# A fourth lead unit in the second auxiliary PSUM pair, and a new order of the work around the leads of four FFNs

## The reference, cut to what matters

```
def swiglu(x, wg, wu, wd):
    return (jax.nn.silu(x @ wg) * (x @ wu)) @ wd

x = x + 0.5 * swiglu(rms_norm(x, n_ffn1[i]), w_ffn1_gate[i], w_ffn1_up[i], w_ffn1_down[i])
mix, v, new_buf, hT = hybrid_mix(rms_norm(x, n_mix[i]), ...)
x = x + mix
x = x + 0.5 * swiglu(rms_norm(x, n_ffn2[i]), w_ffn2_gate[i], w_ffn2_up[i], w_ffn2_down[i])
gate = jax.nn.sigmoid(rms_norm(x, n_ple[i]) @ w_ple_gate[i])
x = x + gate * (p @ w_ple_proj[i])
```

## Time and profile before

| | |
|---|---|
| median of 3 runs | 1858.75 us (1858.49 to 1860.04) |
| the profiled execution: time | 1858.88 us |
| its span, from the first to the last instruction | 1857.2 us |
| mean granted TensorE clock | 0.994 of full speed |
| PE busy | 1819.7 us, 98% of the span |
| DVE busy | 1508.2 us, 81% |
| ACT busy | 1063.0 us, 57% |

### The profile page before, as it was taken

The page is one execution under the profiler, slowest core; times in us unless marked ns, Lnnn a source line. Parts: engine busy times, 40 slices in busy tenths (PEclk is TensorE's granted clock), DMA queues, the critical chain, the costliest instruction groups (busy, mean ns, idle before and its releaser), DMA issues.

```text
span 1857.2 us, 37525 instructions
## 1 busy us (share of the span) xinstructions
PE 1819.7 (98%) x14824; PEld 1797.5 (97%) x14824; DVE 1508.2 (81%) x2319; ACT 1063.0 (57%) x1538; POOL 299.4 (16%) x380
## 2 busy tenths in 40 slices
PE   7999999999999999999999999999999999999997
PEld 6999999998999999999999999999999999999997
DVE  7989978768689889787689789777775897988775
ACT  6656656545456566565466565554544665655553
POOL 0011011340120110112110110115202101011122
PEclk9999999999999999999999999999999999999998
DMA  5657579722346666795355765794223657667941
GB/s 173 155 151 188 136 199 246 216 80 69 110 134 155 175 166 152 194 262 172 124 148 127 197 167 158 209 249 147 71 92 114 162 137 194 158 160 230 237 140 47
DMA packets 81265, 297.16 MB, mean 160 GB/s; under 512 B 9344, under 2 KB 11680, under 8 KB 79312
## 3 DMA queue, kind: packets, MB, share of 16 engines
q1 hardware_dynamic: 52592, 184.87, 30.9%
q0 software_dynamic: 28512, 110.03, 27.8%
HBM read 267.00 MB, written 25.74 MB: 158 GB/s over the span
## 4 chain that ended last, share of the span: by engine, by line
PE 89%; DVE 7%; issue 2%; ACT 1%; DMA 0%; DVEq 0%; SPq 0%; ACTq 0%
PE main L764 24%; PE main L730 19%; PE main L769 12%; PE aux L764 9%; PE main L926 9%; PE aux L769 5%; PE aux L926 4%; PE aux L1028 2%; PE main L819 2%; PE aux L730 1%; PE aux L976 1%; DVE w_lo L1690 1%; PE main L1028 1%; PE aux L1048 0%; DVE tmp L1854 0%
## 5 line engine op out<-in xcount | busy, mean ns | idle before, releaser
L764 PE MATMUL main<-part_hi,w_hi 128*128 128x260 f32 x1296 | 328.5, 284 | 8.8 <-DVE tmp L1854 5.3
L764 PE MATMUL main<-part_lo,w_hi 128*128 128x260 f32 x1296 | 326.6, 283 | 0.0
L764 PEld LDWEIGHTS main<-part_hi,w_hi 128*128 128x128 f32 x1296 | 244.5, 189 | 11.6 <-DVE tmp L1854 7.7
L764 PEld LDWEIGHTS main<-part_lo,w_hi 128*128 128x128 f32 x1296 | 244.5, 189 | 0.0
L622 POOL DMA_DIRECT2D w_lo<-weights_dram x104 | 90.3, 868 | 851.1 <-ACT w_lo L1154 842.5
L769 PE MATMUL main<-part_hi,w_lo 128*128 128x260 f32 x1296 | 213.7, 282 | 0.2 <-DMA w_lo<-weights_dram 0.2
L1166 ACT ACTIVATE w_hi<-tau 128x1024 fp32r<-128x1024 f32 x104 | 109.9, 1057 | 177.0 <-PE main L769 152.4
L730 PE MATMUL main<-part_hi,w_hi 128*128 128x260 f32 x944 | 192.6, 285 | 2.0 <-DVE tmp L1738 2.0
L730 PE MATMUL main<-part_hi,w_lo 128*128 128x260 f32 x944 | 189.8, 283 | 0.0
L730 PE MATMUL main<-part_lo,w_hi 128*128 128x260 f32 x944 | 189.5, 282 | 0.0
L764 PE MATMUL main<-sig,w_hi 128*128 128x260 f32 x1280 | 181.6, 284 | 5.7 <-issue 5.7
(11 more groups left out here) (325 smaller groups left out, 4544.1 us busy)
## 6 DMA issues: line engine op xcount, KB each, us to landing
raw<-weights_dram SPq DMA_DIRECT2D x344, 512.0 KB, 3.8
w_lo<-weights_dram POOLq DMA_DIRECT2D x104, 512.0 KB, 6.4
d_part<-tmp POOLq DMA_DIRECT2D x64, 260.0 KB, 5.3
x<-d_part POOLq DMA_DIRECT2D x16, 1040.0 KB, 14.3
x_spill<-x POOLq DMA_DIRECT2D x6, 1040.0 KB, 4.9
x<-x_spill POOLq DMA_DIRECT2D x6, 1040.0 KB, 9.8
x<-x_in_dram SPq DMA_DIRECT2D x4, 520.0 KB, 6.7
x<-tmp POOLq DMA_DIRECT2D x4, 520.0 KB, 3.2
```

The lines of the kernel that those rows point to most:

```text
L764: pe.matmul(ps, hi_w[:, w], xx(k), start=(start and k == 0 and b == 0), stop=False, skip_group_check=True)
```

## The change

Four things change in the leads and in the first chunk of each FFN.

1. Unit 3 of the lead goes to `aux[1]` (the new list `FOURTHS`). PE waits ahead of it for `root` (`std_s`) and not for `gate_out(0)`. The `main` pairs shift by one, so that P1(0) takes the pair of unit 0 and P1(1) that of unit 1. The wait for `hidden_out(1)` moves from P1(1) to the first down product.
2. On ACT `copy_p1(0)` stands right behind `hi12`, and `h_lead(1)` behind `copy_p5(0)`.
3. On DVE `hidden_out(1)`, `tau3`, `tau4` and `hidden_lo(0)` leave the lead and stand behind `lo12`: `lo12`, `tau3`, `tau4`, `hidden_out(1)`, `lo34`, `hidden_lo(0)`, `lo_b`. `hidden_lo(1)` goes behind `lo12` of the second tile. The copy of the lead's two hidden tiles into x (POOL's queue) becomes two DMAs of one tile each, each behind its own `hidden_out`.
4. The first chunk's sums of pair 0 are made behind tile 0 and not behind tile 2, and the low part of pair 1 moves from tile 1 to tile 2.

```diff
+FOURTHS = tuple(t + 1 for t in THIRDS)
...
-SUM_ORDER = ((1, 0, 2, 3), (0, 1, 2, 3))
...
-    return (g + layer + (k >= G_GT + V_AFTER) + sum(g > t for t in THIRDS)) % 2
+    return (g + layer + (k >= G_GT + V_AFTER) + sum(g > t for t in THIRDS + FOURTHS)) % 2
...
-            return aux[0] if g in THIRDS else main[main_slot(g)]
+            return aux[0] if g in THIRDS else aux[1] if g in FOURTHS else main[main_slot(g)]
...
-            def copy_lead(f, G):
-
-                pool.wait_ge(evac, G)
+            def copy_lead(f, G, k):
+
+                pool.wait_ge(evac, G - 2 * (LEAD - 1 - k))
...
-                pool.dma_start(x[:, XT - 2:XT, :], tmp[:, 2:4, :]).then_inc(lead_copy, 16)
+                pool.dma_start(x[:, XT - LEAD + k, :], T(2 + k)).then_inc(lead_copy[k], 16)
...
                     weights_in(n + 3)
-                    pe.wait_ge(evac, G + 1)
+                    pe.wait_ge(std_s, stat + 1)
                     acc(bank(G + 3), 3, XT, x_hi, x_lo).then_inc(unit, 1)
...
                         if first and t < 2:
-                            pe.wait_ge(evac, G - 2 * (1 - t))
+                            pe.wait_ge(evac, G - 3 + t)
...
-                        if t == 1:
+                        if c and t == 1:
                             pe.wait_ge(evac, G)
...
-                            pe.wait_ge(std_s, stat + 1)
+                            pe.wait_ge(evac, G)
...
                         hi12(n, S)
+                        copy_p1(0)
                         hi34(n, S)
                         act.wait_ge(sx_lo, 2 * KH * (2 * l + which + 1))
                         hi_b(n, S)
-                        h_lead(l, G - 2 * LEAD, 1)
...
-                    copy_p1(0)
+                    if c:
+                        copy_p1(0)
                     copy_p1(1)
                     gate(2)
                     copy_u2(0)
                     copy_p5(0)
+                    if first:
+                        h_lead(l, G - 2 * LEAD, 1)
...
-                            ahead(1, S0, S)
-                            ahead(2, S0, S)
-                            hidden_lo(0)
-                            hidden_out(1)
+                            tau1(S0, S)
+                            tau2(S0, S)
...
-                        if first and t == 2:
+                        if first and t == 0:
                             sums_raw(f, c, 0)
                             sums_raw2(f, c, 0)
...
-                        if not last and t >= pairs and k % 2:
+                        if not last and t >= pairs and k % 2 and not (first and t == 1):
                             sums_lo(l, f, c, k // 2)
                         if first and t == 2:
                             sums_lo(l, f, c, 0)
+                            sums_lo(l, f, c, 1)
...
                     if first:
                         lo12(n, S)
+                        tau_sums(0, (tau3, tau4))
+                        hidden_out(1)
                         lo34(n, S)
-                        dve.wait_ge(hhi, h)
-                        hi_, lo_ = hparts(l)
-                        dve.tensor_tensor(lo_[:, LEAD - 1, :], T(3), hi_[:, LEAD - 1, :], ALU.subtract).then_inc(hlo, 1)
+                        hidden_lo(0)
                         lo_b(n, S)
```

More of the change, by code:

```diff
@@ L136, in first_tile @@
     return TILES * (2 * l + which)
-SUM_ORDER = ((1, 0, 2, 3), (0, 1, 2, 3))
 SUM_AT = ({3: 0, 1: 1, 2: 2, 4: 3}, {1: 0, 3: 1, 2: 2, 4: 3})
 def sums_of(f, c, i):
-    return KH * (DOWN_CHUNKS * f + c) + SUM_ORDER[c].index(i) + 1
+    return KH * (DOWN_CHUNKS * f + c) + i + 1
 def sums_in(f, c):
@@ L309, in trunk @@
         sh_lo = sem("sh_lo")
-        lead_copy = sem("lead_copy")
+        lead_copy = [sem(f"lead_copy{k}") for k in range(LEAD)]
         d_second = sem("d_second")
@@ L667, in gates @@
                         if c == 0 and t == 1:
-                            copy_lead(f, G)
+                            for k in range(LEAD):
+                                copy_lead(f, G, k)
                         if c and t == 1:
@@ L1603, in sums_raw @@
                 if early:
-                    dve.wait_ge(lead_copy, 16 * (f + 1))
+                    for k in range(LEAD):
+                        dve.wait_ge(lead_copy[k], 16 * (f + 1))
                 if f:
@@ L1713, in free @@
                 pending[b] = False
[L1715 to L1724, removed]
             def ffn(l, which, u0, g0):
@@ L1739, in gate_out, with hidden_out @@
                                               ALU.mult).then_inc(evac, 1)
-                        def hidden_out(k):
+                        def hidden_out(k, n=n, G=G, fs=fs):
                             dve.wait_ge(unit, n + 2 * k + 2)
@@ L1745, in hidden_out, with hidden_lo @@
                                               ALU.mult).then_inc(evac, 1)
-                        def hidden_lo(k):
+                        def hidden_lo(k, h=h):
                             dve.wait_ge(hhi, h + k + 1)
@@ L1769, in ffn @@
                             sigma_lo(stat, 3)
-                            tau3(S0, S)
-                            tau4(S0, S)
-                            hidden_lo(0)
                         elif which:
@@ L1824, in c11 @@
                         elif first:
-                            dve.wait_ge(hlo, h)
                             dve.wait_ge(evac, G)
@@ L1851, in c22 @@
                         if first and t < LEAD:
-                            dve.wait_ge(lead_copy, 16 * (f + 1))
+                            dve.wait_ge(hlo, h - LEAD + t + 1)
+                            dve.wait_ge(lead_copy[t], 16 * (f + 1))
                         free(2 + (S + t) % 2)
@@ L1926, in ffn @@
                     lo12(n + 2, S + 1)
+                    if first:
+                        hidden_lo(1)
                     c11_r(0)
```

## The result

| | before | after |
|---|---|---|
| median of 4 runs each | 1859.09 us (1858.49 to 1860.04) | 1871.21 us (1869.31 to 1872.80) |
| the profiled execution: time, span | 1858.88, 1857.2 us | 1872.8, 1871.1 us |
| mean granted TensorE clock | 0.994 | 0.992 |

The kernel is slower by 0.65% (ratio 1.0065, 95% interval 1.005 to 1.008), where 0.55% was forecast. The profiled execution is the longest of the four, so the two traces differ by 13.9 us and the medians by 12.1.

What follows compares the result with a forecast made beforehand. It took PE, busy 98% of the span, to bound the kernel; -0.2 + 2.6 + 0.1 + 2.6 + 6.0 - 0.9 = +10.2 us on 1858.88 gave a forecast of 1869 us, range 1861.5 to 1875.

Steps and rivals of the forecast that it cites:

- The chain: In the leads: tau4(0), load, gate(2), copy_u2(0), P7(0); P7(0) can't start earlier than 6.0 us behind the end of tau4(0).
- Rival C: In the leads: gate(2)'s block lands in time, so P7(0) follows P5(0) without a wait; faster, 1850 us, chance 0.10.
- FFN 1, place of P7(0): Lead of FFN 1: P6(0) starts 4.0 us earlier, but P7(0) only 0.2 us, at 53.3 against 53.53.
- FFN 2, wait at P7(0): Lead of FFN 2: tau4(0) ends 4.2 us later, P7(0) starts at 559.9 against 557.30; +2.6 us.
- FFN 3, place of P7(0): Lead of FFN 3: tau4(0) ends 0.6 us later, P7(0) starts at 966.3 against 966.20; +0.1 us.
- FFN 4, wait at P7(0): Lead of FFN 4: a new wait at P7(0) as in FFN 2, where none was before; +2.6 us.
- clock, four falls: Behind P7(0) in each FFN: clock falls to 0.50 after PE idles, 1.5 us each, +6.0 us in all.
- sums of h: First chunk of each FFN: moved sums shorten the wait for c22(4) by 0.23 us each, -0.9 us in all.
- Stalls of FFN 2 and 4: At P7(0): +2.6 us each, taking 3.7 us from tau4's end to gate(2)'s start, up to 4.7 as bound.
- Rival B: At P7(0): stalls without clock falls in FFN 2 and 4, 1866 us; without any, 1863; chance of 1863 to 1865: 0.10.
- The edits that I costed at nothing: POOL's second small DMA, the moved wait for hidden_out(1), and h_lead(1) and hidden_lo(1) pushing hi12(1) and lo34(1): no cost.

Runs made afterwards that it cites:

- Experiment 1: The changed kernel with tau3 and tau4 of the first tile ahead of lo12 on DVE; 1856.76 us, ratio 0.9984 to the kernel before.
- experiment 2: The changed kernel with gate(2) behind copy_u2(0) and copy_p5(0) on ACT in the first chunk; 1856.18 us, ratio 0.9984 to the kernel before.
- experiment 3: The kernel before with the new bank alone (FOURTHS, slots, PE's waits), ACT and DVE orders as before; 1859.85 us, ratio 1.0004 to the kernel before.
- experiment 5: The changed kernel with tau3 and tau4 ahead of lo12 and gate(2) behind copy_p5(0); 1854.05 us, ratio 0.9972 to the kernel before.
- experiment 6: The changed kernel with 22 unused matmuls more between P5(0) and P7(0) in each lead; 1866.09 us, ratio 1.0036 to the kernel before.
- Experiment 9: The changed kernel with the copy of the lead's second hidden tile issued one tile later; 1868.69 us, ratio 1.0046 to the kernel before.
- Experiment 4: The changed kernel with the sums of h back in their order and places of before; 1872.27 us, ratio 1.0073 to the kernel before.
- Experiment 8: The kernel of experiment 5 with sums_lo(1) moved to the first chunk's end, ahead of down_out(0); 1849.27 us, ratio 0.9948 to the kernel before.

## Why the prediction was right, step by step

**The chain: right, and shown.** The forecast was that the wait removed in FFN 1 and 3 comes back at P7(0), and that FFN 2 and 4 get one that they didn't have, by `tau4(0)`, load, `gate(2)`, `copy_u2(0)`. All four waits stand there, behind `copy_u2(0)`, with ACT idle for the load. Experiment 1 shows the first link (the order of `tau4` and `lo12`), experiment 2 the last (`copy_u2` queued behind `gate(2)`), and experiment 3 that the bank has no part in it. Rival C needed the block in time; it was 2.1 to 2.9 us late. With the chain mended at both links, experiment 5 gives 1854.05 us, 4 us above what C gave for that case. C took the waits for `c22` down by 0.9 from their 5.3 us; in experiment 5 they are 6.9. That is 2.5 of the 4 us; the rest is open. That a shorter lead leaves DVE less time ahead of `c22` would explain the longer waits, but it isn't shown.

**The terms**, in the profiled execution:

| term | forecast | measured |
|---|---|---|
| FFN 1, place of P7(0) | -0.2 | -0.25 |
| FFN 2, wait at P7(0) | +2.6 | +3.52 |
| FFN 3, place of P7(0) | +0.1 | about +0.3 |
| FFN 4, wait at P7(0) | +2.6 | +2.87 |
| clock, four falls | +6.0 | about +8.1 |
| sums of h | -0.9 | -0.8 |
| sum | +10.2 | about +13.7, of 13.9 |

FFN 3 is its displacement of 7.24 us less the 5.52 of FFN 2, less 1.7 for the clock behind P7(0) of FFN 2, plus 0.3 for the shorter wait for `c22(4)` there. The clock is the length of each window of experiment 6 times one less its granted clock, 2.4 + 1.7 + 3.0 + 1.4 = 8.5, less the 0.4 us that were there before: behind P7(0) of FFN 3 the kernel before had a granted clock of 0.78 from 966.20 to 968.00, the end of its own slow stretch. The sums are the 5.0 us of the four waits for `c22(4)` before, less four times 1.05. The -0.25 of FFN 1 has in it that the first wait of the whole run, for `part_lo`, was longer by 0.3 us (8.8 in place of 8.5), which the change doesn't touch. The other terms were read in one execution, which was 1.6 us above its kernel's median; the sum explains that execution, to within 0.2 us.

**Stalls of FFN 2 and 4: mis-sized, by 0.9 and 0.3 us.** I took 3.7 us from the end of `tau4` to `gate(2)`. In FFN 2 it was 560.49 - 555.66 = 4.83, just past the bound of 4.7, and the load itself 4.6. In the place of the one copy of both hidden tiles there are now two, and POOL's queue issued one while this load was in flight. Experiment 9 moved it away, and the load got shorter in all four FFNs, by 0.2, 0.6, 0.3 and 0.4 us. So the copy has a part in it, with one load of each kind. It isn't the whole: in FFN 1 and 3 of the kernel after the copy was in flight too and the load took 3.7 us, and without it that of FFN 2 still took 4.0. The prediction's reading of the earlier trace rows was wrong in this point. It put the 4.5 us of FFN 4 down to the copy, but in FFN 2 of the kernel before, whose load took 3.5, the copy was in flight as well (issued at 551.26, 1.5 us behind the load). What makes one such load 1 us longer than another stays open. The rule of the Trainium skill, "SBUF — State Buffer", section on the DMA setup-cost knee, that was weighed there makes 3.2 us of such a load, an estimate by that page; none of these loads was as short.

**The clock: right in its place, short by 2.1 us.** It fell behind all four stalls, and experiment 6 shows that it is a cost apart from the stall: with the same stall and a busy PE the windows of FFN 1, 2 and 4 are at full clock, and 5.1 us come back. I had taken the slow stretches of the earlier trace rows, 1.5 us each. In FFN 2 and 4 that fits (1.7 and 1.4). In FFN 1 and 3, whose waits are longer (3.95 and 4.76 us), the clock was at or near 0.50 for 5 and 6 us; that it was so because they are longer isn't shown, and the last section has traces against it. PE's busy time grew by less than 8.1 us, by 4.8, since some slow stretches of the kernel before, ahead of P7(0) in FFN 1 and 3, got shorter or went. Rival B, no fall in FFN 2 and 4, didn't happen in the profiled execution. The runs of the kernel after lie between 1869.31 and 1872.80 us, those of the kernel before within 1.55 us; that some of the falls are missing in some of its runs would explain it, but only one of the runs has a trace.

**The sums: right in total.** The waits for `c22(4)` are 1.05 us in all four FFNs, as forecast (near 1.1). In FFN 1, 2 and 4 they came down from 1.36; in FFN 3 the wait was 0.92 before and rose, where 0.23 us less was forecast for each. Experiment 4 shows that edit 4 gives 0.31 us in each FFN. Experiment 8 shows what held the rest: `sums_lo(1)` stood in the same stretch of DVE.

**What nothing shows.** The edits that I costed at nothing have no wait of their own in the trace; they weren't tried one by one.

## What to carry to other kernels

When an edit pulls one wait forward, write down for each engine what is late *next*, and look at the last reader of every buffer slot: an instruction that only frees a slot (`tau4` here) decides when a transfer 3.5 to 4.6 us long can start, and moving it behind an instruction that waits for another engine cost more here than the waits removed. In an in-order stream, an instruction that waits for a transfer belongs behind the short ones that the busiest engine waits for; moving `gate(2)` behind two copies took the late load out of PE's way here. Look first at the places that have no wait before the change: they can only lose, and here they lost 9.6 of 12.1 us.

## What the runs showed of the hardware that was not expected

Waits of PE of nearly the same length went with a fall of the clock and without. Behind 2.50 us (FFN 3 before) and 2.87 us (FFN 4 after) it fell to the lower level, 1.2 GHz. Behind 2.61 us in FFN 3 of experiment 1 and 2.43 us in FFN 4 of experiment 9 it stayed at 2.4 GHz. The windows of these two, of experiment 1

```profile
958.00:968.00 10.00, 7.29 (x58) 7.08 (x59) 9.19 (x16) 5.85 (x11) 1.45 (x2) 1.00 0.81 216
```

and of experiment 9

```profile
1479.00:1484.00 5.00, 3.47 (x28) 3.47 (x29) 3.60 (x7) 3.75 (x7) 1.43 (x2) 1.00 0.89 187
```

have PE idle for 2.7 and 1.5 us of their length (the second begins within the wait) and a clock of 1.00. In FFN 3 of experiment 6 the clock fell behind a wait of only 2.07 us.

What a fall costs doesn't follow the length of the wait either. The wait of FFN 3 took 3.0 us of slow clock with it in the kernel after (a wait of 4.76 us), 1.5 us in experiment 4 (4.63 us) and 1.7 us in experiment 9 (4.51 us), while the shorter wait of FFN 1 in experiment 9 (3.46 us) took 2.8 us. These are the windows of FFN 3 in experiment 4; the first costs 3.89 times 0.39:

```profile
972.11:976.00 3.89, 3.89 (x21) 3.89 (x22) 1.15 (x3) 2.22 (x4) 0.00 (x0) 0.61 0.95 176
976.00:980.00 4.00, 4.00 (x36) 4.00 (x35) 4.00 (x8) 1.86 (x3) 0.00 (x0) 1.00 0.53 164
```

So the length of one stall alone tells neither whether the clock falls nor for how long, and a sum with a fixed price for each stall is uncertain by up to 3 us for every one of them. The Trainium skill, "TensorE: Matmul & The Clock Gate", section "What's actually happening", says that the number of slow matmuls varies with the phase of the gate; these stalls agree with that, but with one trace of each kernel no run here shows it alone.
